# The order in which TensorE streams token columns through the large products of an encoder trunk

## The reference

```
h = h + 0.5 * rms_norm(swiglu(rms_norm(h, g0), gate1, up1, down1), g1)
h = h + rms_norm(mixer(rms_norm(h, g2), w_in, ..., w_out), g3)
h = h + 0.5 * rms_norm(swiglu(rms_norm(h, g4), gate2, up2, down2), g5)

swiglu(x) = (silu(x @ w_gate) * (x @ w_up)) @ w_down      # 1024 -> 2816 -> 1024
```

## Time and profile before

| | |
|---|---|
| Three runs, us | 1942.56, 1948.27 (median), 1949.94 |
| Profiled execution, own time | 1947.21 us |
| Its span, first to last instruction | 1945.3 us |
| Mean granted TensorE clock | 0.99 |
| PE (products) busy | 1909.2 us, 98%, 9136 instructions |
| PE weight loads busy | 1543.7 us, 79% |
| VectorE busy | 1006.3 us, 52% |
| ScalarE busy | 723.1 us, 37% |
| GpSimd busy | 209.9 us, 11% |
| HBM traffic | 96 GB/s over the span |

### The profile page before, as it was taken

The page is one execution under the profiler, slowest core; times in us unless marked ns, Lnnn a source line. Parts: engine busy times, 40 slices in busy tenths (PEclk is TensorE's granted clock), DMA queues, the critical chain, the costliest instruction groups (busy, mean ns, idle before and its releaser), DMA issues.

```text
span 1945.3 us, 24754 instructions
## 1 busy us (share of the span) xinstructions
PE 1909.2 (98%) x9136; PEld 1543.7 (79%) x9136; DVE 1006.3 (52%) x1429; ACT 723.1 (37%) x1134; POOL 209.9 (11%) x433
## 2 busy tenths in 40 slices
PE   8999999999999999999999999999998999999998
PEld 6888888877667888888878888887875778888887
DVE  5664432387657544432376544335876574444323
ACT  4333332255654433332243333223565453333321
POOL 2831000023100000000056100000131000000000
PEclk9999999999999999999999999999998999999999
DMA  6334343351213333343333433333502123333331
GB/s 176 108 106 127 97 119 98 85 158 55 55 46 85 104 95 96 96 118 102 99 89 98 131 98 109 105 94 98 161 25 66 55 86 99 97 97 104 109 90 44
DMA packets 330954, 188.55 MB, mean 97 GB/s; under 512 B 6996, under 2 KB 325432, under 8 KB 329848
## 3 DMA queue, kind: packets, MB, share of 16 engines
q1 hardware_dynamic: 324008, 168.13, 30.1%
q0 software_dynamic: 5824, 18.79, 3.5%
q10 hardware_dynamic: 1040, 0.52, 0.1%
HBM read 175.72 MB, written 11.67 MB: 96 GB/s over the span
## 4 chain that ended last, share of the span: by engine, by line
PE 95%; ACT 2%; DVE 2%; issue 1%; DMA 0%; DVEq 0%; ACTq 0%
PE ps L559 19%; PE ps L561 18%; PE ps L560 18%; PE ps L696 8%; PE ps L695 8%; PE ps L694 8%; PE ps L587 2%; PE ps L588 2%; PE ps L592 2%; PE ps L905 1%; PE ps L882 1%; PE ps L863 1%; DMA raw<-in_ffn_gate 0%; PE ps L639 0%; PE ps L855 0%
## 5 line engine op out<-in xcount | busy, mean ns | idle before, releaser
L1494 DVE TENSOR_TENSOR wl<-raw,wh 128x1024 fp32r<-128x1024 f32 (+1 forms) x265 | 350.6, 1324 | 755.9 <-ACT wh L1046 754.7
L559 PE MATMUL ps<-xh,wh 128*128 128x512 f32 x1552 | 612.4, 395 | 2.4 <-DVEq L1692 1.3
L561 PE MATMUL ps<-xh,wl 128*128 128x512 f32 x1552 | 605.3, 390 | 0.0
L560 PE MATMUL ps<-xl,wh 128*128 128x512 f32 x1552 | 605.2, 390 | 0.0
L1046 ACT ACTIVATE wh<-raw 128x1024 fp32r<-128x1024 f32 (+1 forms) x265 | 301.1, 1137 | 658.7 <-PE ps L696 341.6
L559 PEld LDWEIGHTS ps<-xh,wh 128*128 128x128 f32 x1552 | 292.0, 188 | 67.9 <-issue 3.5
L561 PEld LDWEIGHTS ps<-xh,wl 128*128 128x128 f32 x1552 | 291.8, 188 | 61.6
L560 PEld LDWEIGHTS ps<-xl,wh 128*128 128x128 f32 x1552 | 292.1, 188 | 60.1 <-issue 1.2
L694 PE MATMUL ps<-Hh,wh 128*128 128x512 f32 x704 | 274.0, 389 | 0.0
L696 PE MATMUL ps<-Hh,wl 128*128 128x512 f32 x704 | 273.9, 389 | 0.0
L695 PE MATMUL ps<-Hl,wh 128*128 128x512 f32 x704 | 273.9, 389 | 0.0
(11 more groups left out here) (327 smaller groups left out, 1803.7 us busy)
## 6 DMA issues: line engine op xcount, KB each, us to landing
raw<-in_ffn_up SPq DMA_DIRECT2D x88, 512.0 KB, 3.8
raw<-in_ffn_down SPq DMA_DIRECT2D x64, 704.0 KB, 4.6
raw<-in_ffn_gate SPq DMA_DIRECT2D x87, 512.0 KB, 3.8
raw<-in_w_in SPq DMA_DIRECT2D x28, 512.0 KB, 4.8
raw<-in_w_out SPq DMA_DIRECT2D x16, 512.0 KB, 3.9
xrow<-in_x SPq DMA_DIRECT2D x2, 1024.0 KB, 8.7
ssm_t<-evict POOLq DMA_DIRECT2D x8, 256.0 KB, 3.1
ssm_v<-evict POOLq DMA_DIRECT2D x8, 256.0 KB, 2.7
```

The costliest lines, as they stand in the source:

```text
L559: pe.matmul(bank, w_tile(True, slot, kw), xh[:, kx, :], start=first, stop=False)
L560: pe.matmul(bank, w_tile(True, slot, kw), xl[:, kx, :], start=False, stop=False)
L561: return pe.matmul(bank, w_tile(False, slot, kw), xh[:, kx, :], start=False, stop=last)
L1494: V.tensor_tensor(w_low(slot, k0, nk), raw[:, slot4, 0:nk - k0, :], w_high(slot, k0, nk).bitcast(F32), ALU.subtract).then_inc(w_split, 1)
```

## The change

The 512 columns of a product are read and written in another order, the same for the activations that it reads and for the bank that it writes. In `three` both go from the last column to the first. In the down products each of the three has an order of its own: the first takes columns 256 to 511 and then 0 to 255; the second takes runs of 16 columns, first those at 0, 128, 256 and 384, then those at 16, 144, 272, 400, and so on; the third takes runs of 32 columns, the last run first, ascending within a run. Everything else is the same, the stationary operands too.

```diff
--- before.py
+++ after.py
@@ -525,6 +525,16 @@
 
         @block.tensor
         def _(pe):
+
+            def halves_swapped(t):
+                return t.rearrange("p (a b) -> p a b", a=2)[:, ::-1, :]
+
+            def pieces_strided(t):
+                return t.rearrange("p (a b c) -> p b a c", a=4, b=8)
+
+            def pieces_backwards(t):
+                return t.rearrange("p (a b) -> p a b", b=32)[:, ::-1, :]
+
             pe.sem_inc(unit_done, SPLIT_SLOTS)
             pe.wait_ge(dve_c, 1)
             for _ in range(SPIN_START):
@@ -556,9 +566,9 @@
 
             def three(bank, slot, kw, kx, first, last):
 
-                pe.matmul(bank, w_tile(True, slot, kw), xh[:, kx, :], start=first, stop=False)
-                pe.matmul(bank, w_tile(True, slot, kw), xl[:, kx, :], start=False, stop=False)
-                return pe.matmul(bank, w_tile(False, slot, kw), xh[:, kx, :], start=False, stop=last)
+                pe.matmul(bank[:, ::-1], w_tile(True, slot, kw), xh[:, kx, ::-1], start=first, stop=False)
+                pe.matmul(bank[:, ::-1], w_tile(True, slot, kw), xl[:, kx, ::-1], start=False, stop=False)
+                return pe.matmul(bank[:, ::-1], w_tile(False, slot, kw), xh[:, kx, ::-1], start=False, stop=last)
 
             def unit_x(n, slot, bank, k0=0, nk=KD):
 
@@ -691,9 +701,12 @@
                         slot = down_slot(i)
                         for k in range(KH):
                             f = (i % 2) * KH + k
-                            pe.matmul(bank, wh[:, slot, k, :], Hh[:, f, :], start=(f == 0), stop=False)
-                            pe.matmul(bank, wh[:, slot, k, :], Hl[:, f, :], start=False, stop=False)
-                            mm = pe.matmul(bank, wl[:, slot, k, :], Hh[:, f, :], start=False, stop=(f == KF - 1))
+                            pe.matmul(halves_swapped(bank), wh[:, slot, k, :], halves_swapped(Hh[:, f, :]),
+                                      start=(f == 0), stop=False)
+                            pe.matmul(pieces_strided(bank), wh[:, slot, k, :], pieces_strided(Hl[:, f, :]),
+                                      start=False, stop=False)
+                            mm = pe.matmul(pieces_backwards(bank), wl[:, slot, k, :], pieces_backwards(Hh[:, f, :]),
+                                           start=False, stop=(f == KF - 1))
                         mm.then_inc(unit_done, 1)
 
                 last = l == DEPTH - 1 and f_ffn == 1
```

## The result

The changed kernel takes 1987.23 us (median of 4 runs, 1984.63 to 1992.41) against 1948.3 us for the kernel before: a ratio of 1.0219, 95% interval 1.0193 to 1.0245. It is slower by 39 us, outside the predicted range of 1939 to 1976 us.

A forecast was written before the change was run, and what follows sets the result against it. TensorE, busy for 98% of the span, was taken to bound the kernel, with nothing hiding a longer product. Reversed and down products added 0 + 0 to the profiled 1947.21 us; forecast 1948 us, range 1939 to 1976.

The forecast's parts named there:

- The point from which a change shows: L559 to L561: an extra 2.1 ns a product, from 9.7 us of run spread over 4656 products.
- (a): 4656 reversed products in gate, up and projections: between 0 and +946 us, taken as 0 because neighbouring columns stay adjacent.
- (b): Down products, 704 each of halves, strided and backwards runs: jumps cost 0 to +113 us, taken as 0.
- The lower bound: Reversed products of L559 to L561: 0, since neighbours in time remain neighbours in memory.
- the upper bound: Reversed products: pace of plain-f32 products at L942, 430 ns apart, so +203 ns each, +946 us.
- possible gain: Edited products: at most 11 ns each, 74 us over all, could come back if order caused them; taken as 0.
- Rival 1: L559 to L561: step -1 halves the rate because pairs join only upwards; +946 us, total 2893 us; chance 0.18.
- Rival 2: L694 to L696: every address jump costs a cycle; 27.6 us, 1975 us, or 13.8 us, 1961 us; chance 0.07.
- Rival 4: Whole change: the build folds identical read and write orders into the plain one; 1948 us, inside the no-effect chance 0.72.
- the case as drawn: Whole kernel: range 1939 to 1976 us with a far second peak, nothing expected between 1976 and 2500.
- The rule: Skill page: non-contiguous patterns slow matmuls; read strictly all 6768 products, 3322 us; its next sentence lets every order pass.

The follow-up runs named there:

- the first series: No reference computed; 48 fp32r or bf16 products per read and write order on TensorE alone: fp32r plain 226.6, reversed 233.5, reversed writes 227.0 ns a step.
- `writes_only`: Changed kernel with activations read plainly and only the bank written in the new orders in all six lines: ratio 1.001 to the kernel before.
- the third series: No reference computed; 48-product series with slices 512 columns apart: runs of 64 backwards 226.6, of 32 233.3 to 233.5 ns a step.
- the second: No reference computed; 48-product series varying read starts and pieces, slices 544 columns apart: plain 231.2, reversed 232.4 to 242.2 ns a step.

## Why the prediction was wrong

**What held.** TensorE sets the pace, a product costs its step of 226.7 ns and not its latency, nothing hides a longer one, and no wait, DMA or other engine matters: 36.6 of the 37.5 us by which the span grew are TensorE's busy time, and the six edited lines are the ones that got longer. The point from which a change shows, 2.1 ns a product, was passed. Bank writes in any of the four orders are free, as terms (a) and (b) assumed for them.

**The step that failed: term (a), "I take 0: adjacency is kept".** It measured 6.8 ns a product: 4656 x 6.8 = 31.7 us, and 1.015 alone. The lower bound (0) was an argument about neighbours in memory and the upper one (+203 ns) the pace of another number format, and I took the lower without a row of this format. Even the upper bound was misread: `glu` issues four products a layer at L942 and the trace shows eight records, so 430 ns is one of two records of a plain-float32 product, not a whole one. Adjacency is not what counts. The runs point to how the addresses of the columns run against those of the weights that are loaded meanwhile. Two things in the trace before could have warned me: a weight load begins with each product, and the plain fp32r product was already 11 ns above what bf16's rate gives for 512 columns (226.7 against 215.7). I named those 11 ns only as a possible gain. That they mark a stream without reserve is my reading; bf16, without them, showed none of the price.

**Term (b) failed for two of its three orders.** The rows I leaned on were of the wrong kind. L812 is bf16, and in bf16 strided and backwards pieces cost nothing in the first series either (215.8 ns). The ScalarE rows do not "read the same memory", as I wrote: L1112 reads PSUM, where a product writes, and L1123 writes SBUF, while the price is paid by reads of SBUF. ScalarE also has no weight loads of its own beside them. In fp32r the strided order costs 4 to 5 ns in the series and runs of 32 backwards 6.7. The halves cost nothing of their own (1.0005 in all lines), though L704's latency rose by 4 ns: in the mixed cycle a free order pays beside dear ones. The down part measured 1.004 against my 1.000 in the runs, and 6.1 ns a product against my 0 in the trace.

**The rivals.** Rival 1 had the right place (L559 to L561, step -1) and sign, and a wrong price by a factor of 30: not a halved rate (430 ns) but 3% (233.5 ns), and the read alone. Its mechanism, pairs joined only upwards, is refuted by the writes (227.0 ns) and by the reads in which only each 4 columns were turned (231.2, as plain in the same series). Rival 2, a cycle for every jump, gave the nearest total, 1975 us, by a cause that the runs refute: 7 jumps and 1 jump cost nothing, and 15, 31, 63 and 127 jumps backwards cost the same 6.7 to 6.9 ns. That it came near was luck. Rival 4, orders that never reach the chip, is excluded by the time itself. In the case as drawn, everything between 1976 and 2500 us was declared empty; that gap was the error in the range. A small price per product, times 6768, fell into it.

**The rule.** The Trainium skill's "PSUM Cachelines" ("Advanced Engine Details and Errata"), by its sentence on any non-contiguous pattern, would have slowed the writes; `writes_only` at 1.001 goes against it. The sentence after it, on every two consecutive elements, fits: writes of every second column, which break the pairs, took (20.76 - 0.634)/47 = 428 ns in bf16, and orders that keep the two values of a pair one behind the other, descending ones too, took 216.

**What stays open.** That for plain reads and runs the distance modulo 256 bytes between the columns and the weights decides is shown, in the series and in the kernel, for shifts by multiples of 32 bytes. That the reversed order itself is dear for the same reason fits, but is argued: no layout made it free. That it is a collision in SBUF is my reading. Four results don't follow from it: half the weight columns did not lessen the reversed step, at 256 columns the reversed read had no price, equal shifts by 3 and 4 elements brought nothing back, and a plain product beside a reversed one costs as much as it. What within 256 bytes collides was not tried further. No order or layout beat the plain 226.6 ns, so no version beats the kernel before.

## What to carry to other kernels

In a stream of fp32r products of 512 columns, each with its own weight load, the order in which columns are read was free as long as whole blocks of 64 columns (256 bytes) stayed ascending and the activations kept their distance modulo 256 bytes to the weights. Other orders and distances cost 1 to 3% of a product, and some orders far more; the one exception found is runs of 32 with the two half a block apart (227.0). The distance rule is shown for moves by multiples of 32 bytes; a move of both by 3 or 4 elements did cost. Check the addresses of both tensors modulo 256 after any edit of the SBUF layout: a pad of 32 bytes at the wrong place cost this kernel 2.6%. And when every product is on the path, bound a change in nanoseconds per product, by rows of the same type, before arguing that it is zero.

## What the runs showed of the hardware

- bf16: 216 ns a step at 512 columns in all the orders tried that keep neighbours together. fp32r: 226.6 at best, 233.5 reversed, 229 to 234 with columns or weights shifted alone by 16 bytes to 224 bytes.
- Some fp32r reads are much dearer: pieces of 4 columns (16 bytes) taken in reversed order inside each 16 columns took 266.6 ns in the third series, and strided runs of 16 that started one element off a 16-byte boundary 306.5 ns in the second.
- Every second column read in fp32r took (21.92 - 0.630)/47 = 453 ns, twice the plain step; in bf16 225.8. The Trainium skill's "SBUF Cachelines" ("Advanced Engine Details and Errata") says that SBUF has lines of 16 bytes and that at least two hits on a line are needed to absorb the access latency. This fp32r read has two of the four columns of each line one after the other, and two were not enough.
- A shift of the SBUF layout that moves activations and weights together cost nothing (1.0005 at 32 bytes, 0.9992 at 256).
- A plain fp32r product between two reversed ones takes as long as they do (233.3 ns on average over both).
